# x read feature-major, and the second sequence's x parts and first weight chunk made during the out-projection

## The chip, the cores and the metric

The kernel runs on one core of a Trainium2 chip. The metric is the device time of one execution in microseconds (us), from the first to the last instruction with what lies around it; lower is better.

## The reference

One encoder layer is applied to two sequences of 512 tokens with 1024 features, with the same weights. All arithmetic is float32.

```python
proj = x @ w_in                                  # q, k, v of two kinds of attention, and the gates
ya = gqa_axial_attention(qa, ka, va) @ w_branch_a
yb = dilated_window_attention(...)  @ w_branch_b   # three dilations, with a bias table
merged = g_a * ya + g_b * yb
x  = layer_norm(ALPHA * x + merged @ w_out, ln1_g, ln1_b)
moe = hierarchical_moe(x, ...)                   # 16 experts, 2 of one group for each token
x  = layer_norm(ALPHA * x + moe, ln2_g, ln2_b)
```

## The kernel before

The four engines and SP's DMA queue each run an order of work written out by hand, and wait for each other by semaphores alone. The front (projections, attention, out-projection, first layer norm) is run for sequence 0 and then for sequence 1; then come the routing and the experts of both.

Every float32 operand of a projection is split into a high part (`float32r`, a copy on ScalarE) and a low part (the difference, on VectorE); a product is three matmuls (`mm3`, L660 to L662): high by low, high by high, low by high. The front's weights are 28 chunks of 128x2048 (1 MB), loaded by SP into `raw[c % 2]` (L461, two halves each), split by `split_hi` (L1053) into `whi` and by `split_lo` (L1373) into `wlo`. Chunks 24 to 27 belong to the out-projection; chunk 24 lies in `whi[0]`/`wlo[0]`, chunk 26 in `whi[1]`/`wlo[1]`, the two others elsewhere.

Matmuls contract over the partitions, so x is needed with its features on them, as `xT` (high and low part, 128 x 8 x 512). In the kernel before, a tile of 128 tokens is loaded as rows (`load_x`, L453, 512 KB, into `x_stage[t]`), TensorE turns it by eight transposes against the identity (`turn_x`, L685), ScalarE copies two banks of four to the high part (L1074), and VectorE makes the low part (L1391). Tile 0 of x and chunk 0 come first on SP's queue, then x tiles 1 to 3, then chunk 1. On TensorE the order is: turn tile 0, turn tile 1, project tile 0 by chunk 0, turn tile 2, project tile 1, turn tile 3, project tiles 2 and 3. In sequence 0 there follow six small matmuls that make the bias table (L759; they need the selection rows `sel_sb`, and their results are taken by ScalarE behind the squares of q and by VectorE behind the sum of squares, L1405). Then come chunks 1 to 11. VectorE combines the rope tables (`rope_params`, L1346 to L1354) behind the low part of chunk 1.

The parameters are loaded by ACT's queue at the start (L1032 to L1036): rope 320 KB, front (gate bias and routing weights) 98 KB, route 206 KB, bias 1.5 KB, selection rows 297 KB.

The out-projection runs tile by tile with four chunks of 256 columns each (L910). VectorE adds the residual (L1545) and takes statistics (L1549); after a tile ScalarE takes the root (L1199), and VectorE's `finish(t)` (L1533 to L1536) makes x1 one tile later; TensorE turns x1 (`turn_x1`, L694), ScalarE keeps it (`keep_x1`, L1060), TensorE multiplies it by the routing weights (`route`, L705) and VectorE adds the bias (`logit`, L1379). ScalarE's queue stores x1 (`store_x1`). At the end of sequence 0 the last tile's share of this is done inside sequence 1: `finish(3)` stands ahead of chunk 0's low part on VectorE, and `turn_x1(0, 3)`, `route(0, 2)` and `route(0, 3)` lie between TensorE's first tiles. The merged attention output uses the same `xT` buffers as x, so x's parts of a tile may be written only when the out-projection of that tile is done. SP has x of sequence 1 in `x_stage` and chunks 0 and 1 in `raw` before the out-projection's second tile is through.

## Time and profile before

| | us |
|---|---|
| median of 3 runs | 1425.87 |
| lowest and highest | 1424.17 to 1425.99 |
| the profiled execution | 1428.31 |
| its span | 1426.6 |
| TensorE busy | 1290.1 (90%) |
| VectorE busy | 754.0 (53%) |
| ScalarE busy | 645.9 (45%) |
| GpSimd busy | 270.2 (19%) |

The mean granted clock of TensorE is 0.952 of its full 2.4 GHz. The span is the time from the first to the last instruction; all starts are counted from its start. Busy shares are means over stages with different limits, so a place is read from the timeline and from what ended the idle time there, in brackets behind a row.

### The profile page before, as it was taken

How to read it: one execution, taken by the hardware profiler on the slowest of the kernel's cores; microseconds unless marked ns; L12 is line 12 of the kernel's file. 1: busy time of each engine (PE TensorE's matmuls, PEld its weight loads, DVE VectorE, ACT ScalarE, POOL GpSimd, SP SyncE). 2: the span in 40 equal slices, each digit the busy share in tenths (PEclk: the TensorE clock that was granted, in tenths of full speed). 3: DMA queues.
4: the chain of work that ended last, by engine and by line, in shares of the span. 5: the costliest groups of instructions: out<-in, count | busy, mean ns of one | idle time of the engine just before them, and what ended most of it. 6: DMA issues, size and time to landing. Idle time of an engine off the chain costs nothing.

```text
span 1426.6 us, 20185 instructions
## 1 busy us (share of the span) xinstructions
PE 1290.1 (90%) x7662; PEld 1074.5 (75%) x7663; DVE 754.0 (53%) x957; ACT 645.9 (45%) x878; POOL 270.2 (19%) x279
## 2 busy tenths in 40 slices
PE   5999899999998999999999896488999999999970
PEld 5788767788798888766788796466787778778860
DVE  3333367222654333367212655478855776885556
ACT  3222476332312322466332313367745564875445
POOL 0432000000300332000000300234522433652220
PEclk9999999999999999999999997589999999999995
DMA  7774400144662544300144653289977977996426
GB/s 188 226 169 89 89 1 2 29 90 131 141 201 89 112 96 89 89 2 1 27 93 124 142 207 142 101 269 280 355 218 227 339 248 263 312 378 218 145 74 241
DMA packets 58177, 222.40 MB, mean 156 GB/s; under 512 B 11800, under 2 KB 12312, under 8 KB 50648
## 3 DMA queue, kind: packets, MB, share of 16 engines
q1 hardware_dynamic: 42800, 177.38, 42.0%
q0 software_dynamic: 12192, 34.51, 8.6%
q10 hardware_dynamic: 3116, 9.54, 1.8%
q8 instruction: 50, 0.82, 0.3%
q14 instruction: 19, 0.15, 0.0%
HBM read 200.17 MB, written 34.32 MB: 164 GB/s over the span
## 4 chain that ended last, share of the span: by engine, by line
PE 78%; DVE 8%; issue 6%; ACT 5%; DMA 2%; POOL 1%; ACTq 0%; POOLq 0%; DVEq 0%; SPq 0%
PE banks L660 21%; PE banks L661 20%; PE banks L662 20%; PE banks L830 2%; PE banks L794 2%; PE banks L865 2%; PE banks L944 2%; ACT moe_hi L1211 2%; PE banks L872 1%; DVE moe_lo L1360 1%; PE banks L805 1%; DVE h_full L1706 1%; POOL gated L569 1%; PE banks L969 1%; DMA raw<-in_front_w 1%
## 5 line engine op out<-in xcount | busy, mean ns | idle before, releaser
L1360 DVE TENSOR_TENSOR moe_lo<-moe_raw,moe_hi 128x2048 fp32r<-128x2048 f32 x102 | 233.1, 2289 | 79.5 <-ACT moe_hi L1211 79.1
L1373 DVE TENSOR_TENSOR wlo<-raw,whi 128x2048 fp32r<-128x2048 f32 (+1 forms) x52 | 116.1, 2233 | 185.1 <-ACT whi L1053 185.1
L1211 ACT ACTIVATE moe_hi<-moe_raw 128x2048 fp32r<-128x2048 f32 x102 | 194.7, 1913 | 42.2 <-PE banks L662 39.9
L660 PE MATMUL banks<-xT,whi 128*128 128x512 f32 x448 | 175.4, 391 | 0.0
L661 PE MATMUL banks<-xT,whi 128*128 128x512 f32 x448 | 174.8, 390 | 0.0
L662 PE MATMUL banks<-xT,wlo 128*128 128x512 f32 x448 | 174.8, 390 | 0.0
L660 PE MATMUL banks<-wlo,xT 128*128 128x256 f32 x512 | 149.1, 291 | 8.3 <-DVE xT L1503 7.0
L660 PE MATMUL banks<-moe_lo,xeh 128*128 128x512 f32 x368 | 148.8, 404 | 8.3 <-issue 3.8
L661 PE MATMUL banks<-whi,xT 128*128 128x256 f32 x512 | 146.6, 286 | 0.0
L662 PE MATMUL banks<-whi,xT 128*128 128x256 f32 x512 | 146.5, 286 | 0.0
L661 PE MATMUL banks<-moe_hi,xeh 128*128 128x512 f32 x368 | 145.9, 396 | 0.0
L662 PE MATMUL banks<-moe_hi,xel 128*128 128x512 f32 x368 | 145.8, 396 | 0.0
L1053 ACT ACTIVATE whi<-raw 128x2048 fp32r<-128x2048 f32 (+1 forms) x52 | 95.9, 1845 | 90.6 <-PE banks L662 85.7
L569 POOL TENSOR_TENSOR gated<-gated,kqv 128x512 f32<-128x512 f32 x16 | 25.3, 1594 | 498.3 <-DVE kqv L1519 498.3
L660 PEld LDWEIGHTS banks<-wlo,xT 128*128 128x128 f32 x512 | 100.0, 195 | 11.0 <-DVE xT L1503 8.7
L661 PEld LDWEIGHTS banks<-whi,xT 128*128 128x128 f32 x512 | 100.3, 196 | 0.3
L662 PEld LDWEIGHTS banks<-whi,xT 128*128 128x128 f32 x512 | 100.0, 195 | 0.0
L660 PEld LDWEIGHTS banks<-xT,whi 128*128 128x128 f32 x448 | 84.5, 189 | 18.3 <-issue 0.9
L662 PEld LDWEIGHTS banks<-xT,wlo 128*128 128x128 f32 x448 | 84.4, 188 | 17.6
L661 PEld LDWEIGHTS banks<-xT,whi 128*128 128x128 f32 x448 | 84.6, 189 | 17.3
L614 POOL TENSOR_TENSOR wait_bearer<-wait_bearer 128x1 f32<-128x1 f32 x48 | 45.0, 938 | 269.6 <-DVE y_sb L1730 167.9
L660 PEld LDWEIGHTS banks<-moe_lo,xeh 128*128 128x128 f32 x368 | 70.7, 192 | 26.5 <-issue 9.0
(244 smaller groups left out, 2394.0 us busy)
## 6 DMA issues: line engine op xcount, KB each, us to landing
moe_raw<-in_expert_w SPq DMA_DIRECT2D x192, 512.0 KB
raw<-in_front_w SPq DMA_DIRECT2D x104, 512.0 KB, 6.8
toeplitz_rows<-bias_rows POOLq DMA_DIRECT2D x4, 1152.0 KB, 15.5
kqv<-in_x SPq DMA_DIRECT2D x8, 512.0 KB, 10.7
pt<-in_x SPq DMA_DIRECT2D x2, 2048.0 KB, 9.4
x_rows<-pt ACTq DMA_DIRECT2D x8, 512.0 KB, 2.7
token_sums<-pt ACTq DMA_DIRECT2D x8, 512.0 KB, 3.6
sum_tile<-token_sums SPq DMA_DIRECT2D x8, 512.0 KB, 6.9
```

What stands on the lines that cost most here:

```text
L569: nc.gpsimd.tensor_tensor(gated[:, n, :], gated[:, n, :], sg[:, n, :], ALU.add).then_inc(summed, 1)
L614: return nc.gpsimd.tensor_tensor(wait_bearer[:, 1 + n:2 + n], wait_bearer[:, 0:1], wait_bearer[:, 0:1], ALU.add)
L660: mm(dst, left[0], right[1], start=first, stop=False)
L661: mm(dst, left[0], right[0], start=False, stop=False)
L662: return mm(dst, left[1], right[0], start=False, stop=last)
L794: last = mm(bank[score_bank(p, v)][:, :], qA[halves[v], m, t * P:(t + 1) * P], kA[halves[v], :], start=True, stop=True)
L830: last = nc.tensor.transpose(bank[v][:, j * P:(j + 1) * P], src[:, j * P:(j + 1) * P], ident)
L865: last = mm(dst[v], vA[:, j, v, :], turned[p % 2][v][0][:, j * P:(j + 1) * P], start=(j == 0), stop=(j == 3))
L1053: A(view(w_slot(c)[0], shape), view(raw[c % 2], shape), ACT.Copy).then_inc(w_hi, 1)
L1211: A(moe_hi[m % SPLIT_E], moe_raw[m % RAW_E], ACT.Copy).then_inc(e_hi, 1)
L1360: V.tensor_tensor(moe_lo[m % SPLIT_E], moe_raw[m % RAW_E], moe_hi[m % SPLIT_E].bitcast(F32), ALU.subtract).then_inc(e_lo, 1)
L1373: V.tensor_tensor(view(lo, shape), view(raw[c % 2], shape), view(hi, shape).bitcast(F32), ALU.subtract).then_inc(w_split, 1)
```

## The change

The host gives x a second time, with the features of a tile as rows (`x_turned`, [2, 4, 128, 1024]); `load_x` reads it. The turnings of x, their waits and their banks go. `x_hi` on ScalarE and `x_lo` on VectorE make the two parts from `x_stage`, 128x1024 at a time. For sequence 1 these, and chunk 0's two parts, are placed in the last tiles of sequence 0's out-projection, as the buffers come free (`freed_for`). In sequence 1 `turn_x1(0, 3)` comes between tiles 1 and 2. The parameters are issued by SP: rope, bias and selection rows behind x tiles 1 to 3, the other two behind chunk 2. The wait for the identity moves to the turning of q.

```diff
@@ -156,6 +153,20 @@
 W_FREED = [0, 0] + CHUNK_END[:N_CHUNK - 2]
 W_FREED[C_OUT + 1] = CHUNK_END[C_A - 1]
 W_FREED[C_OUT + 2] = W_FREED[C_OUT + 3] = CHUNK_END[C_OUT - 1]
+LAST_OUT = MM_OUT + N_OUT * (TT - 1)
+
+
+def out_done(t):
+
+    return MM_OUT + N_OUT * (t + 1)
+
+
+def freed_for(c, s):
+
+    if c >= 2 or s == 0:
+        return s * MM_N + W_FREED[c]
+    return (s - 1) * MM_N + LAST_OUT + (1 if c == 0 else 3)
+
 SLOTS = 256
@@ -450,7 +462,7 @@
             for s in range(SEQS):
                 def load_x(t):
                     sp.wait_ge(merged_lo, s * KD + 1)
-                    sp.dma_start(x_stage[t], x_v[bass.ds(s, 1), :, t].rearrange("a i d -> (a i) d")).then_inc(x_in[t], 16)
+                    sp.dma_start(x_stage[t], x_turned[s, t]).then_inc(x_in[t], 16)
                 load_x(0)
                 for c in range(N_CHUNK):
@@ -462,6 +474,13 @@
                     if c == 0:
                         for t in range(1, TT):
                             load_x(t)
+                        if s == 0:
+                            sp.dma_start(rope_t, rope_c).then_inc(rope_in, 16)
+                            sp.dma_start(rel_sb[0:NBUCKET, :], rel_bias).then_inc(sel_in, 16)
+                            sp.dma_start(sel_sb, bucket_sel).then_inc(sel_in, 16)
+                    if s == 0 and c == 2:
+                        sp.dma_start(front_t, front_c).then_inc(const_in, 16)
+                        sp.dma_start(route_t, route_c).then_inc(const_in, 16)
                     if c == C_A - 1:
                         sp.wait_ge(mm_done, s * MM_N + MM_GATE + 1)
@@ -676,15 +693,6 @@
                         name, value = turned_by(TR_ORDER[i - 2])
                         pe.wait_ge(by_name[name], value)
                     return bank[i % 2]
-
-                def turn_x(t):
-                    pe.wait_ge(x_in[t], s * 16 + 16)
-                    for f in range(2):
-                        b = tr_open(("x", s, t, f))
-                        for k in range(4):
-                            last = nc.tensor.transpose(b[:, k * P:(k + 1) * P],
-                                                       x_stage[t][:, (4 * f + k) * P:(4 * f + k + 1) * P], ident)
-                        last.then_inc(tr_done, 1)
                 def turn_x1(seq, t):
                     pe.wait_ge(x1_ready, seq * TT + t + 1)
@@ -733,22 +741,18 @@
                     return last
                 def qkv_tile(t):
-                    pe.wait_ge(xlo, s * 2 * TT + 2 * t + 2)
+                    pe.wait_ge(xlo, s * TT + t + 1)
                     by_token(0, t, t, xT_v)
-                turn_x(0)
-                if s > 0:
-                    turn_x1(s - 1, 3)
-                turn_x(1)
                 qkv_tile(0)
                 if s > 0:
                     route(s - 1, 2)
-                turn_x(2)
                 qkv_tile(1)
                 if s > 0:
+                    turn_x1(s - 1, 3)
+                qkv_tile(2)
+                if s > 0:
                     route(s - 1, 3)
-                turn_x(3)
-                qkv_tile(2)
                 qkv_tile(3)
                 if s == 0:
                     pe.wait_ge(sel_in, 32)
@@ -767,6 +771,7 @@
                 pe.wait_ge(tab_act, N_TAB // 2)
                 pe.wait_ge(tab_dve, N_TAB // 2)
                 pe.wait_ge(q_turned, s * 3 + 3)
+                pe.wait_ge(ident_in, 16)
                 for t in range(TT):
                     b = tr_open(("q", s, t))
                     for m in range(4):
@@ -1029,12 +1034,6 @@
         def _(act):
             A = nc.scalar.activation
-            act.dma_start(rope_t, rope_c).then_inc(rope_in, 16)
-            act.dma_start(front_t, front_c).then_inc(const_in, 16)
-            act.dma_start(route_t, route_c).then_inc(const_in, 16)
-            act.dma_start(rel_sb[0:NBUCKET, :], rel_bias).then_inc(sel_in, 16)
-            act.dma_start(sel_sb, bucket_sel).then_inc(sel_in, 16)
-
             for s in range(SEQS):
                 def mm_wait(n):
                     act.wait_ge(mm_done, s * MM_N + n + 1)
@@ -1045,10 +1044,16 @@
                     act.wait_ge(tr_done, i + 1)
                     return bank[i % 2]
-                def split_hi(c):
+                def x_hi(seq, t):
+                    act.wait_ge(x_in[t], seq * 16 + 16)
+                    if seq > 0:
+                        act.wait_ge(mm_done, (seq - 1) * MM_N + out_done(t))
+                    A(xT_v[0][:, :, t * P:(t + 1) * P], x_stage[t].rearrange("p (k n) -> p k n", k=KD), ACT.Copy).then_inc(xhi, 1)
+
+                def split_hi(c, s=s):
                     shape = chunk_shape(c)
-                    act.wait_ge(mm_done, s * MM_N + W_FREED[c])
+                    act.wait_ge(mm_done, freed_for(c, s))
                     act.wait_ge(raw_in[c % 2], (s * (N_CHUNK // 2) + c // 2) * 32 + 32)
                     A(view(w_slot(c)[0], shape), view(raw[c % 2], shape), ACT.Copy).then_inc(w_hi, 1)
@@ -1065,20 +1070,16 @@
                     act.dma_start(x1_d[seq * SEQ + t * P:seq * SEQ + (t + 1) * P, :], xr[:, t, :]).then_inc(x1_out, 16)
                     act.dma_start(acc_d[seq * SEQ + t * P:seq * SEQ + (t + 1) * P, :], xr[:, t, :]).then_inc(acc_out, 16)
-                if s > 0:
+                if s == 0:
+                    x_hi(0, 0)
                     split_hi(0)
-                    act.wait_ge(mm_done, s * MM_N)
-                for t in range(TT):
-                    for f in range(2):
-                        b = tr_wait(("x", s, t, f))
-                        A(xT_v[0][:, 4 * f:4 * f + 4, t * P:(t + 1) * P], b.rearrange("p (k n) -> p k n", k=4), ACT.Copy) \
-                            .then_inc(xhi, 1)
-                    if s == 0 and t == 0:
-                        split_hi(0)
-                    if s > 0 and t == 0:
-                        store_x1(s - 1, 3)
-                        keep_x1(s - 1, 3)
-                split_hi(1)
+                    for t in range(1, TT):
+                        x_hi(0, t)
+                    split_hi(1)
+                else:
+                    split_hi(1)
+                    store_x1(s - 1, 3)
+                    keep_x1(s - 1, 3)
                 for c in range(N_QKV):
                     n0, q = MM_QKV[c], QKV[c]
                     if q < 3:
@@ -1193,12 +1194,18 @@
                         split_hi(2 * c + C_OUT - 2 * C_A)
                         split_hi(2 * c + C_OUT - 2 * C_A + 1)
                 for t in range(TT):
+                    if s + 1 < SEQS and t == 3:
+                        split_hi(0, s + 1)
                     if t >= 1:
                         store_x1(s, t - 1)
                     act.wait_ge(ln_var, s * TT + t + 1)
                     A(rstd1[:, t:t + 1], rstd1[:, t:t + 1], ACT.Sqrt).then_inc(ln_root, 1)
                     if t >= 1:
                         keep_x1(s, t - 1)
+                        if s + 1 < SEQS:
+                            x_hi(s + 1, t - 1)
+                if s + 1 < SEQS:
+                    x_hi(s + 1, 3)
                 if s == SEQS - 1:
                     store_x1(s, 3)
                     keep_x1(s, 3)
@@ -1366,7 +1373,13 @@
                     dve.wait_ge(mm_done, s * MM_N + n + 1)
                     return bank[mm_bank(n)]
-                def split_lo(c):
+                def x_lo(seq, t):
+                    dve.wait_ge(xhi, seq * TT + t + 1)
+                    cols = slice(t * P, (t + 1) * P)
+                    V.tensor_tensor(xT_v[1][:, :, cols], x_stage[t].rearrange("p (k n) -> p k n", k=KD),
+                                    xT_v[0][:, :, cols].bitcast(F32), ALU.subtract).then_inc(xlo, 1)
+
+                def split_lo(c, s=s):
                     shape = chunk_shape(c)
                     dve.wait_ge(w_hi, s * N_CHUNK + c + 1)
                     hi, lo = w_slot(c)
@@ -1379,22 +1392,18 @@
                     V.tensor_tensor(logits[:, (seq * TT + t) * 20:(seq * TT + t + 1) * 20], bank[6 + t % 2][:, 0:20],
                                     b_route, ALU.add).then_inc(logit_ready, 1)
-                if s > 0:
+                if s == 0:
+                    x_lo(0, 0)
                     split_lo(0)
-                for t in range(TT):
-                    if s > 0 and t >= 2:
-                        logit(s - 1, t)
-                    if s == 0 and t == 1:
-                        split_lo(0)
-                    for f in range(2):
-                        dve.wait_ge(xhi, s * 2 * TT + 2 * t + f + 1)
-                        V.tensor_tensor(xT_v[1][:, 4 * f:4 * f + 4, t * P:(t + 1) * P],
-                                        bank[TR_ORDER.index(("x", s, t, f)) % 2].rearrange("p (k n) -> p k n", k=4),
-                                        xT_v[0][:, 4 * f:4 * f + 4, t * P:(t + 1) * P].bitcast(F32), ALU.subtract) \
-                            .then_inc(xlo, 1)
-                split_lo(1)
-                if s == 0:
+                    for t in range(1, TT):
+                        x_lo(0, t)
+                    split_lo(1)
                     rope_params()
+                else:
+                    x_lo(s, 3)
+                    split_lo(1)
+                    logit(s - 1, 2)
+                    logit(s - 1, 3)
                 for c in range(N_QKV):
                     n0, q = MM_QKV[c], QKV[c]
                     if q < 3:
@@ -1549,11 +1558,17 @@
                         ins = V.bn_stats(stats[:, o:o + 6], xr[:, t, col])
                         if c == 0 and t >= 1:
                             finish(t - 1)
+                        if s + 1 < SEQS and c == 2 and t >= 2:
+                            x_lo(s + 1, t - 2)
+                        if s + 1 < SEQS and c == 1 and t == 3:
+                            split_lo(0, s + 1)
                         if c == 2 and t == 3:
                             logit(s, 0)
                     chain(ins)
                     chain(V.bn_aggr(mv[:, 2 * t:2 * t + 2], stats[:, t * N_OUT * 6:(t + 1) * N_OUT * 6]))
                     V.tensor_scalar(rstd1[:, t:t + 1], mv[:, 2 * t + 1:2 * t + 2], LN_EPS, None, ALU.add).then_inc(ln_var, 1)
+                if s + 1 < SEQS:
+                    x_lo(s + 1, 2)
                 finish(3)
                 logit(s, 1)
                 if s == SEQS - 1:
@@ -1846,7 +1861,10 @@
     nc = _bacc.Bacc("TRN2", target_bir_lowering=False, num_devices=1)
     arrays = {"x": _np.concatenate([_np.asarray(inputs["x_prompt"]), _np.asarray(inputs["x_sample"])], 0),
+              "x_turned": None,
               "front_w": front_chunks(*[_np.asarray(inputs[n]) for n in ("w_in", "w_branch_a", "w_branch_b", "w_out")])}
+    arrays["x_turned"] = _np.ascontiguousarray(
+        arrays["x"].reshape(SEQS, P, TT, KD, P).transpose(0, 2, 4, 3, 1)).reshape(SEQS, TT, P, D)
     for n in _INS:
         if n == "ln2_g":
             arrays["expert_w"] = expert_chunks(*[_np.asarray(inputs[n]) for n in ("w_expert_in", "w_expert_out")])
```

## Rows read from the trace of the kernel before

**Rows 1.** The page's part 4: the chain that ended last, share of the span by engine.

```profile
PE 78%; DVE 8%; issue 6%; ACT 5%; DMA 2%; POOL 1%; ACTq 0%; POOLq 0%; DVEq 0%; SPq 0%
```

**Rows 2.** Timeline of TensorE, 14 to 40 us. Columns: start us, us, engine, line, operation, tiles, count, idle before.

```profile
17.96 0.55 PE L660 MATMUL banks<-wlo,xT 128*128 128x256 f32 x1 [1.35 <-DVE wlo L1373]
...
22.77 1.03 PE L685 MATMUL banks<-ident,kqv 128*128 128x128 f32 x8
...
23.56 0.36 PE L660 MATMUL banks<-wlo,xT 128*128 128x256 f32 x1
...
33.22 1.88 PE L759 MATMUL banks<-pt,rel_bias_rows 33*4 33x512 f32 x4
...
39.54 0.79 PE L660 MATMUL banks<-xT,whi 128*128 128x512 f32 x1
```

**Rows 3.** Timeline of ScalarE and VectorE, 13 to 36 us.

```profile
13.58 1.91 ACT L1053 ACTIVATE whi<-raw 128x2048 fp32r<-128x2048 f32 x1 [4.91 <-DMA raw<-in_front_w]
...
15.53 2.29 DVE L1373 TENSOR_TENSOR wlo<-raw,whi 128x2048 fp32r<-128x2048 f32 x1 [6.13 <-ACT whi L1053]
...
32.27 0.42 DVE L1346 TENSOR_TENSOR cos_k<-rope_params 128x256 f32<-128x256 f32 x1
...
34.83 1.22 DVE L1405 TENSOR_REDUCE ss<-prob 128x16 f32<-128x1024 f32 x1 [0.77 <-ACT prob L1097]
```

**Rows 4.** DMA view, 0 to 13.5 us: queue, packets, MB, share of 16 engines (q1 SP's, q10 ACT's).

```profile
q1 hardware_dynamic: 599, 2.23, 59.7%
...
q10 hardware_dynamic: 524, 0.94, 25.9%
```

**Rows 5.** DMA view of L461, 1.5 to 3 us: its two issues until landing, us.

```profile
DMA to landing us min/median/max: 8.2/9.6/11.1
```

**Rows 6.** Stretch view, one microsecond. Columns: busy us PE, PEld, DVE, ACT, POOL, clock, DMA share, GB/s.

```profile
3.00:4.00 1.00, 0.00 (x0) 0.00 (x0) 0.00 (x0) 0.43 (x1) 0.00 (x0) 1.00 1.04 396
```

**Rows 7.** DMA view, 4.7 to 7 us: the next chunk's two issues, KB each, us to landing.

```profile
raw<-in_front_w SPq DMA_DIRECT2D x2, 512.0 KB, 17.8
```

**Rows 8.** Timeline of TensorE, 439 to 469 us.

```profile
439.38 1.04 PE L694 MATMUL banks<-ident,pt 128*128 128x128 f32 x8
...
441.96 1.07 PE L685 MATMUL banks<-ident,kqv 128*128 128x128 f32 x8
...
447.06 1.94 PE L694 MATMUL banks<-ident,pt 128*128 128x128 f32 x8 [4.03 <-DVE xT L1391]
...
448.93 1.94 PE L685 MATMUL banks<-ident,kqv 128*128 128x128 f32 x8
...
450.52 0.56 PE L660 MATMUL banks<-wlo,xT 128*128 128x256 f32 x1
...
454.24 1.86 PE L705 MATMUL banks<-front_params,gated 128*128 128x20 f32 x16
...
455.94 1.07 PE L685 MATMUL banks<-ident,kqv 128*128 128x128 f32 x8
...
456.78 0.37 PE L660 MATMUL banks<-wlo,xT 128*128 128x256 f32 x1
...
468.10 0.40 PE L660 MATMUL banks<-xT,whi 128*128 128x512 f32 x1
```

**Rows 9.** Timeline of ScalarE, 441 us.

```profile
441.09 1.07 ACT L1060 ACTIVATE gated<-banks 128x512 f32<-128x512 f32 x2
```

**Rows 10.** Timeline of VectorE, 422 to 443 us.

```profile
422.52 0.42 DVE L1545 SCALAR_TENSOR_TENSOR pt<-pt,banks 128x256 f32<-128x256 f32 x1 [1.38 <-PE banks L662]
...
425.40 0.42 DVE L1545 SCALAR_TENSOR_TENSOR pt<-pt,banks 128x256 f32<-128x256 f32 x1 [2.00 <-PE banks L662]
...
441.42 1.29 DVE L1535 SCALAR_TENSOR_TENSOR pt<-pt,mv,kqv 128x1024 f32<-128x1024 f32 x1
```

**Rows 11.** Stretch view of two stretches, columns as in Rows 6.

```profile
441.96:450.52 8.56, 4.53 (x26) 3.95 (x26) 5.52 (x6) 4.64 (x7) 0.00 (x0) 0.70 0.67 201
...
468.10:590.00 121.90, 121.90 (x762) 110.61 (x761) 39.12 (x34) 33.29 (x42) 29.66 (x48) 1.00 0.48 104
```

More of the change, by code:

```diff
@@ L70 @@
     for _t in range(TT):
-        TR_ORDER += [("x", _s, _t, f) for f in range(2)]
         if _s > 0 and _t == 0:
@@ L129, in turned_by @@
 def turned_by(key):
-    if key[0] == "x":
-        return "xlo", 2 * TT * key[1] + 2 * key[2] + key[3] + 1
     if key[0] == "x1":
@@ L185, in __call__, with encoder_kernel @@
         self.eng.wait_ge(self.sem, self.n)
-def encoder_kernel(nc, x, front_w, rel_bias, ln1_g, ln1_b, expert_w, ln2_g, ln2_b, rope_c, front_c,
+def encoder_kernel(nc, x, x_turned, front_w, rel_bias, ln1_g, ln1_b, expert_w, ln2_g, ln2_b, rope_c, front_c,
                    route_c, bucket_sel, ident_c, out):
     x_v = x.rearrange("s (i c) d -> s i c d", c=TT)
+    assert x_turned.shape == (SEQS, TT, P, D)
     out_v = out.rearrange("s (i c) d -> s i c d", c=TT)
@@ L662, in mm3 @@
                 return mm(dst, left[1], right[0], start=False, stop=last)
-            pe.wait_ge(ident_in, 16)
             for s in range(SEQS):
```

## The prediction

> **What bounds the kernel now.** I read first the page's chain, then the timeline of TensorE at the two places that the change touches, then the timelines of ScalarE and VectorE and the DMA view there. The chain lies on TensorE for 78% of the span, and 6% more is issue [rows 1]: an edit pays only where it takes work or waiting off TensorE. There are two such places: the start, before the second weight chunk is multiplied, and the boundary between the sequences.
>
> At the start TensorE's first projection matmul is at 17.96 us, released by the low part of chunk 0 on VectorE [rows 2]. Behind that stand the 2.29 us of that subtraction and the 1.91 us of the high part on ScalarE, which itself waited until 13.58 for the transfer of chunk 0 [rows 3]. So the start is a transfer: its two halves take 8.2 and 11.1 us to land [rows 5]. From 17.96 TensorE is busy until the bias-table matmuls at 33.22, and the second chunk starts at 39.54 [rows 2].
>
> At the boundary the out-projection's last routing matmuls end at 441.96, where the first turning of x begins. Then TensorE idles 4.03 us, turns x1 and the next x tile at half pace (8 turnings take 1.94 us, where the same 8 took 1.04 at 439.38), and starts the first projection tile only at 450.52. The second chunk starts at 468.10 [rows 8]. The mean granted clock from 441.96 to 450.52 is 0.70, that is partly the 1.2 GHz level [rows 11]. The idle time ends with VectorE's low part of x (the row names L1391): VectorE is still in finish(3), which begins at 441.42 [rows 10], and then has chunk 0's subtraction ahead of it.
>
> **The change part by part, at the start.** (a) The parameters leave ACT's queue. Up to 13.5 us that queue moved 0.94 MB and took 25.9% of the 16 engines' time, that is 0.259 x 13.5 = 3.5 us; SP's queue took 59.7% [rows 4]. In the new order identity, x tile 0 and chunk 0 stand ahead of everything in the one queue that is left, x tiles 1 to 3, rope, bias and selection rows behind it, and the other two parameter blocks behind chunk 2. So chunk 0 lands 3.5 us earlier, at 10.0, and 13.58 - 3.5 + 4.38 (from ScalarE's start to the first matmul, 13.58 to 17.96, unchanged) gives a first matmul at 14.46. Bounds: if the engines that ended last held little of the parameters, 1.5 us; if the queue alone reaches the rate of the fourth microsecond, 396 GB/s [rows 6], the 1.64 MB up to chunk 0 take 4.1 us from about 2.6 (0.06 identity, 0.52 x, 1.05 weights), land near 7 to 8, and the gain is 5.5 to 6.5. I take 3.5.
>
> The Trainium skill ("DMA: Bandwidth & Descriptors", Specifications) gives about 358 GB/s of HBM per core. By that figure as an estimate chunk 0 would land at 2.6 + 1.64/0.358 = 7.2 us and the first matmul would be 6.3 us earlier. The same skill ("Trainium Kernel Development and Optimization", Key Constraints) says that the queues of SP, ACT and POOL share the same 16 DMA engines and that several issuers save only issue time: by it the move of parameters as such gains nothing, and only the order does.
>
> (b) The x turnings go. In sequence 0 two of the four tiles' turnings lie between projection tiles: from 22.77 to 23.56 = 0.79 us each, 1.58 in all [rows 2]. The other two lie before the first matmul, in waiting time, and are worth nothing. What replaces them is one ScalarE copy of 128x1024 per tile (half of 1.91 = 1.0 us) and one VectorE subtraction (half of 2.29 = 1.15 us) [rows 3]. Tile 0's parts are made while chunk 0 is on its way; those of tiles 1 to 3 lie behind chunk 0's split and beside 4 tiles of matmuls of about 3 us. TensorE's stretch at 1.2 GHz is inside tile 0 (4.81 us, from 17.96 to 22.77) and moves with it; if it lasts longer because no turnings run ahead of it, each microsecond costs half: bound 0 to 1 us, taken at 0.
>
> (c) What may be late next. The second chunk now has rope and selection rows (0.6 MB) ahead of it in the queue, but 0.3 MB of others not beside it. It landed 17.8 us after its issue at about 5 us, near 23 [rows 7], and should land at 22 to 23 again. ScalarE waits for it in its order, with the copies of q behind it, and VectorE's rope parameters stand behind its subtraction: 23 + 1.9 + 2.3 + 1.8 = 29.0 (the rope parameters run from 32.27 to 34.06, where the idle 0.77 before 34.83 begins). The reduction that gates the tables starts, as now, 1.6 us after the tables' first matmul (34.83 against 33.22) [rows 2, 3]; that matmul moves to 14.46 + (33.22 - 17.96 - 1.58) = 28.1, the reduction to 29.7. So it just fits; a chunk landing at 25 would cost 1.3 us. The table stage itself, 33.22 to 39.54 = 6.3 us, keeps its length. The start gains 3.5 + 1.58 = 5.1 us. The rest of sequence 0 is shifted by it.
>
> **At the boundary.** From 441.96 to 468.10 TensorE takes 26.14 us [rows 8]. Removed: first turnings and the idle behind them, 441.96 to 447.06 = 5.10; x tile 1's turnings, 448.93 to 450.52 = 1.59; tiles 2 and 3, 455.94 to 456.78 = 0.84, twice. Sum 8.37. The x1 turning moves between tiles 1 and 2 and runs warm: 1.87 (447.06 to 448.93) becomes 0.87, a gain of 1.00. Tile 0 runs warm: 3.72 (450.52 to 454.24) becomes 2.95, a gain of 0.77. Sum 10.1 us; 16.0 are left: four tiles of about 2.9, two routings of 1.70 (454.24 to 455.94), one turning. The cold clock disappears because its cause, the idle, does.
>
> Who pays: VectorE and ScalarE, inside the out-projection. VectorE waits 1.38 and 2.00 us before each of the residuals of a tile [rows 10]. Tile 2 takes one x subtraction of 1.15 before the residual at 425.40: hidden. Tile 3 takes chunk 0's subtraction (2.29) and x tile 1's (1.15) into gaps of 1.4 and 2.0, so its last statistics end about 0.3 us late. Then x_lo(1,2) stands before finish(3). It waits for ScalarE, which first keeps x1 (1.07 us from 441.09 [rows 9]), then copies x tile 2: done at 443.5. The subtraction ends at 444.7, finish(3) (2 x 1.3 us and a reciprocal) at 447.5. TensorE needs it for turn_x1(0,3), after tile 0, a routing and tile 1, at 441.96 + 2.95 + 1.70 + 2.95 = 449.6: slack 2.1 us. Tile 2 wants x_lo(1,2) at 450.4 (ready 444.7); the second routing wants x1T at 453.4, tile 3 x_lo(1,3) at 455.1 (about 449), the second chunk its split at 458 (about 452). ScalarE's wait for chunk 0's slot (until the last tile's first group, about 431) has only the store of x1 tile 2 behind it, which waits for about 434 anyway. SP's queue is not changed in order here. All is hidden; price if VectorE is 3 us late: about 1 us of idle.
>
> **Sum.** 5.1 + 10.1 = 15.2 us. Nothing later has a fixed time: from 468.10 to 590 TensorE is busy throughout at clock 1.00 [rows 11], and the expert loads start from the last splits, which move along. The profiled execution took 1428.31 (span 1426.6 us), the runs have a median of 1425.87. So: profiled 1413.1, span 1411.4, median 1410.7.
>
> **The rivals.** Chunk 0 at full rate: for it speaks the 396 GB/s of the fourth microsecond, against it that SP's queue moved only 2.23 MB in 13.5 us with 59.7% of the engines [rows 4, 6], that is 2.23/(0.597 x 13.5) = 277 GB/s. It gains 2.5 more: 1408.2. Waits take the place of the turnings at the boundary: VectorE's line above has 2.1 us of slack by my sums; if ScalarE or VectorE come 4 to 5 us late, TensorE idles 2 to 3 us and runs part of a tile at 1.2 GHz: 1413.7. The start gives little: chunk 0 moves by 1.5 us, or the second chunk or selection rows come late and gate the tables; 3 us less: 1413.7 to 1414.2. Other side: the clock. The pause at the boundary goes, and out-projection and projections become one dense stretch of some 190 us; if TensorE were granted 1.2 GHz somewhere in it, each microsecond there loses half. 15.2 + 2.9 us are eaten from 36 us of it on, at say 44 us the time is 1410.7 + 22 = 1432.7. Against it: 122 us of the present projections run at 1.00 [rows 11]. That the change does not do what it says: x is read turned by rows of the same size as before, so only a transfer could differ, and all of the second sequence's land long before use; no chance of its own.
>
> **How the numbers follow.** Forecast 0.60 (own range 1409 to 1412.5); full rate 0.15; waits at the boundary 0.12; little at the start 0.09; the clock 0.04, half of it with a time within 0.2%. The range 1407.3 to 1414.3 takes in the forecast, the full rate and the better halves of the two middle ones. A measurement of this kernel tells about 0.2% (2.9 us) from no change. Faster by more: 0.96; within: 0.02; slower: 0.02.
>
> **What would show it.** First projection matmul at 14.5 us, second chunk at 34.4; between the last routing of the out-projection and the first projection tile of sequence 1 no idle, the interval to the second chunk 16.0 us, granted clock 1.00 in it; VectorE's finish(3) before 449.6 less 5.1. Wrong if chunk 0 lands outside 8 to 12 us, if TensorE waits on the x subtractions or on x1 at the boundary, or if the tables' matmuls wait on the selection rows.

## The result, and the profile after

| | before | after |
|---|---|---|
| median, us | 1425.38 (1424.17 to 1425.99) | 1403.38 (1402.7 to 1406.52) |
| the profiled execution | 1428.31 | 1403.19 |
| its span | 1426.6 | 1401.5 |

Four runs of each on one chip; the ratio is 0.9849, with a 95% interval of 0.9833 to 0.9865, that is 22 us less (19 to 24). The forecast was 15.2 us less, and the time lies 3.9 us below the range. The sign was right, the size was not.

From the page of the kernel after: the span, the busy time of TensorE, and the queue that brings instructions. TensorE is still 74% of the chain of work, so the same engine bounds the kernel.

```profile
span 1401.5 us, 20036 instructions
PE 1269.2 (91%) x7598; PEld 1056.1 (75%) x7599; DVE 752.2 (54%) x949; ACT 644.2 (46%) x870; POOL 270.6 (19%) x279
q8 instruction: 49, 0.80, 0.2%
PE 74%; DVE 8%; issue 6%; DMA 5%; ACT 4%; POOL 2%; SPq 0%; ACTq 0%; POOLq 0%; DVEq 0%
```

**The start.** TensorE's timeline after (start, duration, engine, line, operation; in brackets the idle time ahead and what ended it). The first projection matmul, the bias-table matmuls and the second chunk answer to [rows 2], the ScalarE and VectorE rows to [rows 3], the landing to [rows 5].

```profile
15.43 0.55 PE L679 MATMUL banks<-wlo,xT 128*128 128x256 f32 x1 [15.43 <-DVE wlo L1386]
...
28.98 1.88 PE L763 MATMUL banks<-pt,rel_bias_rows 33*4 33x512 f32 x4
31.08 1.02 PE L763 MATMUL banks<-pt,rel_bias_rows 33*4 33x512 f32 x2 [0.23 <-ACT qkvA L1103]
33.29 2.72 PE L763 MATMUL banks<-pt,rel_bias_rows 33*4 33x256 f32 x6 [1.19 <-DVE qkvA L1420]
35.93 0.79 PE L679 MATMUL banks<-xT,whi 128*128 128x512 f32 x1
```

```profile
11.05 1.91 ACT L1058 ACTIVATE whi<-raw 128x2048 fp32r<-128x2048 f32 x1 [4.04 <-DMA raw<-in_front_w]
...
25.37 1.91 ACT L1058 ACTIVATE whi<-raw 128x2048 fp32r<-128x2048 f32 x1 [9.56 <-DMA raw<-in_front_w]
```

```profile
27.31 2.29 DVE L1386 TENSOR_TENSOR wlo<-raw,whi 128x2048 fp32r<-128x2048 f32 x1 [8.62 <-ACT whi L1058]
29.52 0.42 DVE L1353 TENSOR_TENSOR cos_k<-rope_params 128x256 f32<-128x256 f32 x1
...
31.23 1.21 DVE L1414 TENSOR_REDUCE ss<-prob 128x16 f32<-128x1024 f32 x1
```

```profile
DMA to landing us min/median/max: 6.3/7.4/8.5
```

The last line is chunk 0's two halves: 6.3 and 8.5 us from issue to landing instead of 8.2 and 11.1. The first matmul comes 2.53 us earlier and the second chunk 3.61 earlier. Chunk 1 lands later than hoped (ScalarE waits for it until 25.37), so the reduction that gates the last of the tables starts at 31.23, 2.25 behind the tables' first matmul, and TensorE idles 1.19 ahead of them.

**The boundary.** TensorE after, from the last x1 turning of the out-projection, and one row of the windows (stretch, its length, busy time and count by engine, granted clock, DMA share, GB/s). They answer to [rows 8] and [rows 11].

```profile
437.43 1.86 PE L713 MATMUL banks<-front_params,gated 128*128 128x20 f32 x16
439.14 0.36 PE L679 MATMUL banks<-wlo,xT 128*128 128x256 f32 x1
...
442.09 1.86 PE L713 MATMUL banks<-front_params,gated 128*128 128x20 f32 x16
...
446.75 1.03 PE L702 MATMUL banks<-ident,pt 128*128 128x128 f32 x8
```

```profile
439.14:455.15 16.01, 16.01 (x138) 16.01 (x138) 7.56 (x9) 5.91 (x9) 0.00 (x0) 1.00 0.58 154
```

TensorE goes from the routing into the projection without a gap: 16.01 us to the second chunk, all of it busy, clock 1.00, against 26.14 before. This repeats: all seven profiled kernels with before's boundary take 26.14 to 26.29, all six with after's 16.01 or 16.02. VectorE's side, which was to pay for it:

```profile
440.32 1.23 DVE L1379 TENSOR_TENSOR xT<-kqv,xT 128x1024 fp32r<-128x1024 f32 x1 [2.19 <-ACT xT L1051]
...
442.97 1.28 DVE L1545 SCALAR_TENSOR_TENSOR pt<-pt,rstd,kqv 128x1024 f32<-128x1024 f32 x1
```

The subtraction of x waits for ScalarE's copy, as the prediction had it, and `finish(3)` ends at 442.97 + 1.28 = 444.25; TensorE asks for x1 at 446.75. The slack is 2.5 us (2.1 forecast).

**What is left over.** These two places make 3.6 + 10.1 = 13.7 of the 25.1 us between the two profiled executions. Between them, inside sequence 0, the kernel after takes 0.8 more (39.54 to 441.96 before, 35.93 to 439.14 after). The rest, some 12 us, lies behind 590 us, where no line of the change stands. The windows below part it: from the second sequence's last projections to the first expert step's matmuls, and from there over the first expert steps. Before, then after:

```profile
596.64:939.17 342.53, 303.23 (x1987) 248.70 (x1987) 172.24 (x309) 142.79 (x244) 24.98 (x23) 0.90 0.33 98
939.17:981.37 42.20, 32.68 (x150) 25.92 (x148) 33.65 (x29) 28.71 (x29) 8.98 (x9) 0.92 0.89 291
```

```profile
583.50:920.50 337.00, 297.15 (x1987) 243.12 (x1987) 172.22 (x309) 142.61 (x244) 24.96 (x23) 0.92 0.34 99
920.50:954.66 34.16, 29.99 (x149) 24.01 (x148) 30.77 (x27) 25.92 (x26) 11.20 (x9) 1.00 0.94 326
```

The same work takes 5.5 us less in the first stretch and 8.0 us less in the second. Behind the second 1.6 are given back (981.37 to 1426.6 is 445.2 us, 954.66 to 1401.5 is 446.8), so from the first expert step to the end it is 6.4 less. In the second, TensorE before stood still twice, and between the two it ran at a clock of 0.75 (955.32 to 966.22). TensorE's timeline before at the two stops:

```profile
951.12 0.40 PE L662 MATMUL banks<-moe_hi,hT 128*128 128x512 f32 x1
955.32 0.79 PE L660 MATMUL banks<-moe_lo,xeh 128*128 128x512 f32 x1 [3.79 <-issue]
...
978.15 0.40 PE L662 MATMUL banks<-moe_hi,hT 128*128 128x512 f32 x1
981.37 0.79 PE L660 MATMUL banks<-moe_lo,xeh 128*128 128x512 f32 x1 [2.82 <-DVE moe_lo L1360]
```

The same place after has one short stop:

```profile
934.10 0.49 PE L679 MATMUL banks<-moe_lo,xeh 128*128 128x512 f32 x1 [1.26 <-issue]
```

The first stop ends with "issue": TensorE waited for nothing that the profile shows. The second is put down to VectorE's subtraction for `moe_lo`, which ended at 980.57, 0.8 us ahead and 2 us after the stop began. A run below (32 matmuls that never run) shows that the matmul does not wait for it: there the same subtraction runs from 970.06 to 972.35, and TensorE starts the same matmul at 970.26. The DMA view of before shows something else there, an instruction transfer of 16 KB (0.02 MB in the rows) on queue q8. Its rows for 951.5 to 952.0 and for 977.0 to 977.5 are:

```profile
DMA packets 25, 0.11 MB, mean 213 GB/s; under 512 B 2, under 2 KB 2, under 8 KB 24
## 3 DMA queue, kind: packets, MB, share of 16 engines
q1 hardware_dynamic: 24, 0.09, 54.4%
q8 instruction: 1, 0.02, 11.8%
...
q1 hardware_dynamic: 34, 0.09, 47.0%
q8 instruction: 1, 0.02, 12.0%
```

TensorE goes on 3.3 to 3.8 and 3.9 to 4.4 us after these two half microseconds. After the change such a transfer falls into 930.0 to 930.5 and TensorE goes on at 934.10, again about 4 us later, but it had work until 932.8.

Such transfers are no rarity. The DMA view of before, 27 to 905 us:

```profile
q8 instruction: 44, 0.72, 0.4%
```

These are 44 transfers for 5509 matmuls and 5508 weight loads (250 instructions for each), and not one stop of TensorE above 0.8 us ends with "issue" there. Behind 983 us there is no such transfer, though the experts go on for 440 us: by then their loop has been gone through once. Both stops stand at the first matmul of an expert, and there the code is not straight: the loop (L1017 to L1025) has two versions of an expert's step, for 128 and for 256 slots, and goes over the one that it doesn't take. The version that these experts take has 92 matmuls; the other has 168 by its code, with their loads 336 instructions.

### The profile page after: what moved, and what is told of

It reads as the page before. It is cut to its first block, busy times and chain, and to the rows that moved or that the text cites. A ratio compares the mean times of both kernels' runs of the same rounds, so it can differ in the third digit from the quotient of the medians.

```text
span 1401.5 us, 20036 instructions
## 1 busy us (share of the span) xinstructions
PE 1269.2 (91%) x7598; PEld 1056.1 (75%) x7599; DVE 752.2 (54%) x949; ACT 644.2 (46%) x870; POOL 270.6 (19%) x279
## 4 chain that ended last, share of the span: by engine, by line
PE 74%; DVE 8%; issue 6%; DMA 5%; ACT 4%; POOL 2%; SPq 0%; ACTq 0%; POOLq 0%; DVEq 0%
PE banks L679 20%; PE banks L681 19%; PE banks L680 19%; PE banks L835 2%; PE banks L799 2%; PE banks L870 2%; DMA moe_raw<-in_expert_w 2%; PE banks L877 1%; PE banks L949 1%; DMA raw<-in_front_w 1%; ACT moe_hi L1218 1%; DVE moe_lo L1367 1%; DMA token_sums<-y_sb,slot_ids 1%; PE banks L810 1%; POOL gated L588 1%
## 5 line engine op out<-in xcount | busy, mean ns | idle before, releaser
L633 POOL TENSOR_TENSOR wait_bearer<-wait_bearer 128x1 f32<-128x1 f32 x48 | 49.7, 1035 | 262.5 <-DVE y_sb L1745 146.6
```

What stands on the lines that cost most here:

```text
L633: return nc.gpsimd.tensor_tensor(wait_bearer[:, 1 + n:2 + n], wait_bearer[:, 0:1], wait_bearer[:, 0:1], ALU.add)
```

## The theories

Two stretches of unchanged code became faster. Theory **code**: TensorE's instructions come in blocks of 16 KB; by taking 64 turnings out, the change moved the expert loop against these blocks, so a block is asked for earlier against the work that covers it. Rival **memory**: the new input array moves the others in memory, and the experts' weights load better. Rival **time**: the expert phase falls differently against the transfers because all before it is shorter. Rival **start and boundary**: these two places give more than their stretches show, or not what they show.

The count of instructions tells how large the shift is. Before has 7662 matmuls and 7663 weight loads, after 7598 and 7599: 128 instructions less, and 49 transfers on q8 instead of 50. (The waits that go with the turnings are not counted here.)

## Experiments

Every ratio is to the kernel before, run beside it on the same chip (medians 1424.98, 1425.44 and 1425.79 in the three groups). Times stand as median (lowest to highest).

**Before with 64 small matmuls at TensorE's start.** It moves the code without touching anything else, was meant to lie in waiting time, and was taken for half a block.

```diff
             pe.wait_ge(ident_in, 16)
+            for _n in range(64):
+                mm(bank[7][:, 0:8], ident, ident[:, 0:8], start=True, stop=True)
```

> The kernel before with 64 matmuls of 8 columns added at TensorE's start, where it waits for chunk 0 anyway; nothing else. What is open: the changed kernel gained 12.1 us more in its profiled execution behind the second sequence's first chunk, most of it at the first two experts. Theory 'code': TensorE's instructions arrive in blocks of 16 KB (256 instructions of 64 bytes, queue q8), and the change takes 128 instructions out ahead of the experts, so that the block boundary no longer falls where TensorE has just used up its code. Adding 128 moves it by the same half block: the 3.8 us stall at the second expert shrinks to about 1, and the time falls by 6 to 9 us, to 1416 to 1420. Theory 'memory' (a new input moves the expert weights in HBM) and theory 'phase' (the tail depends on the clock time at which it starts): no change, 1425 +- 1.5.

Measured: 1445.6 (1443.6 to 1446.44), ratio 1.0136 [1.0111, 1.0161]. The row of the 64 and the first turning behind them:

```profile
4.45 27.48 PE L667 MATMUL banks<-ident 128*128 128x8 f32 x128 [4.45 <-DMA ident<-in_ident_c]
31.78 1.95 PE L687 MATMUL banks<-ident,kqv 128*128 128x128 f32 x8
```

They took 27.5 us, 0.43 each, and so were not hidden: the first projection matmul came at 38.63, 20.7 us late, which is the whole difference of the medians. The first expert steps took 41.8 us (42.2 before), so nothing moved there. The page explains why: 7790 matmuls and 7791 weight loads, 256 instructions more, and 51 transfers on q8 instead of 50. Each of these float32 matmuls is two matmuls and two loads in the trace, so sixty-four are just one block, and whatever follows lies against the blocks as it did. Both the time and the half block of the expectation were wrong; the run tests theory code only in so far as a whole block was to change nothing, and it gave the block's size.

**After with the same 64.** The same edit ahead of the first projection.

> The changed kernel with the same 64 small matmuls at TensorE's start, so that the code ahead of the experts is again as long as before. 'Code': the stall at the second expert comes back, time 1409 to 1413. 'Memory' and 'phase': 1403.4 +- 1.5 (the matmuls end before chunk 0 is split).

Measured: 1415.91 (1413.72 to 1422.67), ratio 0.9949 [0.9929, 0.9968]. The first matmul came 14.65 us late, the second chunk 13.5; the first expert steps took 33.0 us, without a stop, as in the kernel after. One block more brings no stop here either; the expected return of the stop rested on the same wrong half block.

**Before with the new input array, unused.**

```diff
     arrays = {"x": ...
+              "x_spare": None,
...
+    arrays["x_spare"] = _np.ascontiguousarray(
+        arrays["x"].reshape(SEQS, P, TT, KD, P).transpose(0, 2, 4, 3, 1)).reshape(SEQS, TT, P, D)
```

> The kernel before with the turned x as a further input that nothing reads, in the same place among the inputs. 'Memory': the expert loads run at the rates of the changed kernel and the time falls by 6 to 9 us, to 1416 to 1420. 'Code' and 'phase': 1425 +- 1.5.

Measured: 1423.18 (1419.99 to 1428.28), ratio 0.9986 [0.9968, 1.0005]. That is at most 4.6 us by the interval, and 1.8 by the median, and both stops are there (2.35 and 4.37 us): the theory memory falls as an account of 8 us.

**After with the parameters on ACT's queue again.** The five transfers are issued at ScalarE's start as before, the rest is the change.

```diff
-                        if s == 0:
-                            sp.dma_start(rope_t, rope_c).then_inc(rope_in, 16)
...
+            act.dma_start(rope_t, rope_c).then_inc(rope_in, 16)
+            act.dma_start(front_t, front_c).then_inc(const_in, 16)
...
```

> The changed kernel with the five parameter transfers back on ACT's queue at the start. The recorded prediction gives the move 3.5 us; the trace of the changed kernel shows the first projection matmul at 15.43 instead of 17.96 us, so 2.5. Expected: first projection matmul at 17.5 to 18, time 1405 to 1407; if the parameters had nothing to do with it, 1403.4.

Measured: 1405.29 (1403.68 to 1413.78), ratio 0.9855 [0.9831, 0.9878]. The first matmul and the second chunk:

```profile
18.29 0.55 PE L672 MATMUL banks<-wlo,xT 128*128 128x256 f32 x1 [18.29 <-DVE wlo L1385]
...
37.88 0.80 PE L672 MATMUL banks<-xT,whi 128*128 128x512 f32 x1
```

The first matmul is 2.86 us later than in the kernel after, the second chunk 1.95, and the median is 1.9 us higher. The profiled execution was the longest of the five (1413.78), and it shows a stop at the experts, though TensorE has the instructions of the kernel after:

```profile
943.84 0.79 PE L672 MATMUL banks<-moe_lo,xeh 128*128 128x512 f32 x1 [3.82 <-issue]
```

**Before with the parameters on SP's queue.** That part of the change alone.

```diff
+                        if s == 0:
+                            sp.dma_start(rope_t, rope_c).then_inc(rope_in, 16)
...
-            act.dma_start(rope_t, rope_c).then_inc(rope_in, 16)
...
```

> The kernel before, with only the parameters moved to SP's queue. The reverse of the run with the parameters back on ACT's queue, which moved the first projection matmul by 2.9 us. Expected 2 to 3 us below the kernel before at the second chunk; in all 1422 to 1423. If the queue of the parameters is what shortens the tail: 1415.

Measured: 1422.42 (1419.0 to 1426.46), ratio 0.9981 [0.9965, 0.9998].

```profile
15.79 0.55 PE L667 MATMUL banks<-wlo,xT 128*128 128x256 f32 x1 [1.42 <-DVE wlo L1375]
...
37.77 0.79 PE L667 MATMUL banks<-xT,whi 128*128 128x512 f32 x1
```

The first matmul comes 2.17 us earlier, the second chunk 1.77; the median is 3.0 us lower. With the run before it: the move of the parameters is worth 2 to 3 us at TensorE's first matmuls, added or taken away. The totals agree, but that of the run before it overlaps the kernel after.

**After with the second sequence's x parts and chunk 0 made at its start.** They go back to where before has them; the turned input stays.

```diff
                 else:
+                    split_hi(0)
+                    for t in range(TT):
+                        x_hi(s, t)
                     split_hi(1)
...
-                        if s + 1 < SEQS:
-                            x_hi(s + 1, t - 1)
```

(and the same on VectorE)

> The changed kernel, but x parts and chunk 0 of the second sequence are made at its start, behind the out-projection, as before. This separates the reading of x (nothing turned, parameters on SP's queue) from the early parts. The recorded sums give the whole boundary 10.1 us; here TensorE waits behind the out-projection for finish(3), chunk 0's low part and x tile 0's: 441.2 + 2.8 + 2.3 + 1.2 = 447.5 against 439.1 free, so 8 to 9 us idle and about 2 us of the lower clock. Expected 1403.4 + 10 to 11 = 1413.5 to 1414.5. If the early parts are what shortens the experts as well (the tail of the changed kernel is some 8 us shorter than the boundary and the start explain), 1420 or more.

Measured: 1408.65 (1407.19 to 1416.78), ratio 0.9898 [0.9867, 0.993], 5.3 us above the kernel after. TensorE at the boundary, and the window from the x1 turning to the second chunk:

```profile
435.73 1.86 PE L713 MATMUL banks<-front_params,gated 128*128 128x20 f32 x16
442.98 0.58 PE L679 MATMUL banks<-wlo,xT 128*128 128x256 f32 x1 [5.39 <-DVE xT L1376]
```

```profile
434.85:461.29 26.44, 21.05 (x162) 20.95 (x161) 13.39 (x16) 10.57 (x14) 0.00 (x0) 0.87 0.46 120
```

The stage is 26.44 us, against 18.59 with the parts made ahead and 28.72 before. So of the boundary's 10.1 us, 7.85 are the placing (5.39 of idle, the rest clock: 0.87 instead of 1.00), and only 2.3 are the turnings that are no longer there. In the total that execution's start was 2.1 us shorter, which leaves the 5.7 that it took longer. The stretch carries what the total shows, so the boundary gives no more than its 10.1 us. The expectation (8 to 9 us of idle, 10 to 11 in the total) was too high: it put the whole of the boundary's gain down to the placing.

**Before with 32 matmuls that never run, ahead of the expert loop.** Half a block of code, jumped over.

```diff
             passes = pe.value_load(n_pass[0:1, 0:1], min_val=1, max_val=4)
+            with pe.If(passes > 3):
+                for _n in range(32):
+                    mm(bank[7][:, 0:8], ident, ident[:, 0:8], start=True, stop=True)
```

> The kernel before with 32 matmuls behind a condition that never holds, placed ahead of the expert loop in TensorE's code: nothing more is executed, but the loop's code lies further on in its 16 KB blocks. The stalls at the first expert steps (3.79 us with no releaser at 955.32 in the kernel before, and 2.82 at 981.37) end 3.6 to 4.1 us behind a transfer of queue q8. Theory 'code': the stalls change with the place, time 3 to 8 us away from 1425 in at least one of the two kernels with skipped code. Theory 'clock': the tail is shortened only by where the lower clock falls, no change, 1425 +- 2.

Measured: 1416.93 (1415.63 to 1417.38), ratio 0.9937 [0.992, 0.9954]: 8.5 us less than the kernel before, with nothing changed that is computed. Its two windows:

```profile
598.24:937.23 338.99, 298.38 (x1986) 243.98 (x1987) 172.15 (x309) 142.64 (x244) 24.95 (x23) 0.92 0.34 100
937.23:970.26 33.03, 30.20 (x150) 23.93 (x148) 30.63 (x27) 25.82 (x26) 12.84 (x8) 1.00 0.91 305
```

The first expert steps take 33.0 us instead of 42.2, at clock 1.00, and TensorE stops ahead of neither of the two experts' first matmuls (the 1.4 us that it waits once an expert for VectorE's `h_full` stand in every kernel). VectorE's subtraction beside the second of them, at 970.26:

```profile
970.06 2.29 DVE L1363 TENSOR_TENSOR moe_lo<-moe_raw,moe_hi 128x2048 fp32r<-128x2048 f32 x1
```

It ends 2.1 us behind that matmul's start, so in before it wasn't what the second stop waited for.

**The same with 64, a whole block.**

> As with 32, but 64 matmuls skipped. 'Code': a time other than the kernel before's by 3 to 8 us in this one or the other. 'Clock': 1425 +- 2 in both.

Measured: 1424.71 (1420.62 to 1426.27), ratio 0.999 [0.9973, 1.0007]. 51 transfers on q8, stops of 2.67 and 4.65 us, and:

```profile
934.70:976.60 41.90, 31.68 (x149) 25.19 (x148) 35.48 (x30) 30.46 (x31) 13.72 (x10) 0.93 0.89 295
```

Twice the code, no gain. So it is not the added jump that helps, but the place in the block.

**Before with 64 turnings that never run.** The very instructions that the change takes out (128, half a block), added once more.

```diff
+            with pe.If(passes > 3):
+                for _n in range(64):
+                    nc.tensor.transpose(bank[7][:, 0:P], ident, ident)
```

> The kernel before with 64 transposes (as many as the change takes out) behind a condition that never holds, ahead of the expert loop in TensorE's code. 32 skipped matmuls took 8.5 us off the kernel before and 64 nothing, as if 64 matmuls were one whole block of code. Theory 'code': the change's 64 transposes are about half such a block, so putting them in instead of taking them out also shifts by half: 1415 to 1418. If the change's own gain in the tail has another cause than the length of the code: no shift by half, anything near 1425 is as likely.

Measured: 1417.71 (1414.1 to 1420.41), ratio 0.9945 [0.9925, 0.9965], 8.1 us less; the first expert steps take 33.0 us (12.27, 8.48 and 12.28 for the three parts of which before took 16.15, 10.90 and 15.15).

**After with the same 64.** It gives back the code that the change took out, at the experts' side.

> The changed kernel with 64 skipped transposes at the same place, which brings the loop's code back to where it lies in the kernel before. 'Code': the stalls come back and the time rises by 6 to 9 us, to 1409.5 to 1412.5. Otherwise: 1403.4 +- 1.5.

Measured: 1411.22 (1408.07 to 1413.37), ratio 0.989 [0.9852, 0.9928], 7.8 us above the kernel after (6 by the two ratios). The two stops, and its windows:

```profile
936.01 0.40 PE L681 MATMUL banks<-moe_hi,hT 128*128 128x512 f32 x1
940.09 0.79 PE L679 MATMUL banks<-moe_lo,xeh 128*128 128x512 f32 x1 [3.68 <-issue]
...
966.38 0.79 PE L679 MATMUL banks<-moe_lo,xeh 128*128 128x512 f32 x1 [2.98 <-DVE moe_lo L1370]
```

```profile
581.73:924.07 342.34, 303.40 (x1986) 248.85 (x1987) 172.19 (x309) 142.78 (x244) 24.97 (x23) 0.90 0.34 98
924.07:966.38 42.31, 32.75 (x150) 25.96 (x148) 33.80 (x29) 28.87 (x29) 8.96 (x9) 0.92 0.89 292
```

The stops are those of before to a tenth or two (3.79 and 2.82), though the whole front is that of the kernel after and the expert phase begins 15 us earlier. That ends the rival time: 15 us earlier the stops stand, and in before with 32 matmuls that never run, where the phase begins 2 us earlier, they are gone. Instruction transfers fall into 936.0 to 936.5 and 962.0 to 962.5; TensorE goes on 3.6 to 4.1 and 3.9 to 4.4 us later.

**After with 32 and with 16 matmuls that never run** (half a block and a quarter, the edit of above).

> The changed kernel with 32 skipped matmuls, the step that helped the kernel before. 'Code': here it does the opposite and costs 6 to 9 us, 1409.5 to 1412.5. If a skipped branch by itself hid the stalls (its jump makes a block arrive earlier): 1403 or less.

> The changed kernel with 16 skipped matmuls, a quarter of a block. No size is forecast: it shows whether the effect has steps in between. 'Code': between 1400 and 1412. Otherwise 1403.4 +- 1.5.

Measured: 1408.51 (1407.24 to 1413.05), ratio 0.9886 [0.9847, 0.9926], with stops of 2.31 and 4.44 us; and 1404.85 (1403.82 to 1405.58), ratio 0.9852 [0.9817, 0.9887], with one of 4.26. Two stops cost 5 us over the kernel after here; one costs 1.5, which the spread of the runs does not tell from nothing. The kernel after was measured on another chip than these three, so the sizes are less sure than their direction: all eight times with two stops (1407.24 to 1413.37) lie above all four of the kernel after (1402.7 to 1406.52).

## Why the prediction was wrong

**The step that failed** is "Nothing later has a fixed time". It looked at the stretch from 468.10 to 590, which is unchanged as said (128.5 us before, 128.4 after), and took the rest as shifted. The expert steps were not: they are the same instructions at other places of a 16 KB block, and the first steps of their first pass lost 8.0 us in the trace of before that they do not lose after (6.4 by the end of the span). Shown in both directions: half a block more takes 8.1 to 8.5 us off before, and puts 5.1 to 7.8 on after; a whole block more takes away no stop of before (two runs) and brings none to after (one run). It isn't the only thing that decides. The first expert steps took 39.7 to 42.3 us in six executions that have before's placing (its own, a block or other work added, or the turnings given back to after), and 33.0 to 34.2 in three that have after's, but 39.3 in the fourth, with one stop (after with the parameters on ACT's queue). So after's placing mostly avoids the stops, not always. What differs is when the transfer comes: 9.8 and 10.0 us into the first expert steps in two executions of after's code, 11.0 to 11.4 in four of before's, but 12.2 to 12.4 in three, that of before, the turnings given back, and this fourth. In these three it starts only as TensorE runs out of work. What delays it is not shown. Nor did a run test whether the stops need the jump over the other version of the step: that rests on where they stand. The trace of before had the signs, two stops of TensorE of 3.79 us on "issue" and 2.82 us, a clock of 0.75 between them, and an instruction transfer at each; the prediction did not look at that place, because no line of the change is there. It had no rival for it.

**The sum with that term.** Without the placement the change is worth about 1425.8 - 1411.2 = 14.6 us (10 to 21 by the interval), where 15.2 were forecast. With both kernels placed without stops it comes to about the same: 13.5 to 14.3 from before with half a block more (1416.93 and 1417.71) to after (1403.38).

**The boundary** was right in size, mechanism and slack: 16.01 us for 16.0, clock 1.00, 10.1 us gained, and no wait in place of the turnings. The rival of waits there did not come.

**The start** was 5.1 in the forecast and 3.6 in the profiled pair. Single executions differ there by a microsecond: in five executions whose start is that of before the first matmul comes at 17.57 to 18.42, mean 17.97, and the second chunk at 38.11 to 40.55, mean 39.29; in five with the start of after (the profiled one and four of the experiments) at 14.50 to 15.43, mean 14.91, and 33.85 to 35.93, mean 34.63. So (a), 3.5 us, measured 3.1, and the start 4.7 for 5.1. Term (b), the two turnings, held: from the first matmul to the tables' first it is 15.40 in the mean before and 13.67 after, 1.7 for 1.58. Term (c), the tables unchanged, held in the mean and missed in the profiled execution: there chunk 1 was split from 25.37 and not from 23, the reduction came at 31.23 and not 29.7, and the table stage took 6.95 us and not 6.3; the means of the same executions are 5.9 before and 6.0 after. The price named there for a chunk landing at 25 was 1.3 us; 0.65 was paid, since the reduction gates only the later tables.

The Trainium skill ("DMA: Bandwidth & Descriptors", Specifications) gives about 358 GB/s of HBM per core, by which as an estimate chunk 0 would have been there at 7.2 us. It was ready at 11.05 (issued at 1.8 and 2.4, 6.3 and 8.5 us to land): the measurement decides against the figure here. The rival of the full rate fell too. The DMA view of after, 2.5 to 11.0 us:

```profile
q1 hardware_dynamic: 428, 2.06, 96.7%
```

SP's queue had the engines nearly to itself and moved 2.06 MB in these 8.5 us, 242 GB/s and not 396. "Trainium Kernel Development and Optimization" (Key Constraints) says that the queues share the same engines; the two runs on the parameters agree so far as order alone, 2 to 3 us, is what their move brings.

**The clock** as a rival did not come: the out-projection and the projections behind it run at 1.00 through the boundary.

**Added up**: 4.7 at the start, less about 0.7 inside sequence 0 (in the means of the same executions), 10.1 at the boundary and 6.4 from the first expert step to the end make 20.5, against 22.0 measured in the medians. What is open is the stretch of 5.5 us from 596.64 to 939.17, which for the most part is not the change's. It took 342.5 us in before's profiled execution, but 337.0 to 339.3 in six other executions of before's code (with what was added to it); with the code of after it took 336.2 to 337.2 in five executions and 342.3 and 342.5 in two. So either code now and then takes 3 to 6 us more there, at a granted clock of 0.90 instead of 0.92 or 0.93. The three long ones are the three executions in which the experts' transfer came latest; what links the two stays open. Among the short ones alone the first expert steps still took 39.7 to 41.9 with before's placing and 33.0 to 34.2 with after's, so the placing does not hang on it.

## What to carry to other kernels

An edit that removes or adds instructions moves all code behind it, and where TensorE meets code for the first time a stop of up to 4.7 us may come or go (here at the experts alone, behind a piece of code that it goes over, and nowhere in straight code): look in the profile for idle time that ends with "issue", or with a releaser that was done earlier, and for an instruction transfer just ahead of it. Before a gain is put down to the edit, give the removed instructions back as code that never runs; it takes one run, and here it parted 14.6 us from 7.8. Work that only prepares operands belongs ahead of a boundary even where the engines that do it seem idle enough behind it: 7.85 of the boundary's 10.1 us were that placing, and 2.3 the work removed.

## What the runs showed of the hardware

- TensorE's instructions arrive in transfers of 16 KB (50 of them, 0.82 MB) on the queue q8, during the run: one for each 250 matmuls and loads from 27 to 905 us, none behind 983 us, where the experts' loop repeats. 128 matmuls with 128 weight loads are one more of them. The Trainium skill ("Trainium Architecture — The Big Picture", The software stack) gives 64 bytes an instruction, by which as an estimate 256 are 16 KB: the trace agrees.
- In all 16 stops of over 2 us at the experts that the profiles show, one such transfer falls 3.3 to 4.6 us ahead of TensorE's next instruction. The stop is what is left of these 4 us when the work that TensorE already has is done. All 16 stand at the first matmul of an expert; the 44 transfers from 27 to 905 us brought none. That the instruction beyond the block is what TensorE waits for is inferred from this and from the half-block and whole-block runs; the profile names none, or VectorE's subtraction, for which the matmul does not wait.
- The experts' loop holds 1040 matmuls and loads (two experts, each in both versions, by its code). It is repeated for 440 us without one more transfer, so code that was brought once is not brought again.
- A stop costs more than its length: before, two stops of 6.6 us together cost 9.2 against the kernel with 32 matmuls that never run; the clock behind the first was 0.75 instead of 1.00.
- Small float32 matmuls of 128x8 at the very start took 0.43 us for each call (two passes each), so sixty-four of them are no free filler.
